# Two transformer blocks on one core: in block 1's attention the projections are dealt to the steps by a written plan, and the gating of an output moves ahead of them on VectorE

## The chip, the cores and the metric

One Trainium2 chip, one of its cores. The metric is the device time of one execution in microseconds. One execution was profiled; all rows come from it.

## What is computed

The reference runs two blocks on one sequence of 1024 tokens with 1024 features, each of two layers. The change touches the attention of block 1, which a layer has twice:

```python
def diff_attention(q, k, v, lam):            # branch "a": 4 heads of two halves of 64
    s = einsum(q, k) / sqrt(d); mask = kpos <= qpos
    p = softmax(s)
    pd = p[:, :, 0] - lam * p[:, :, 1]
    return einsum(pd, v)                     # then a norm, and the gate silu(z)
# branch "c": 8 heads of 64, partial_rope on q and k, three dilated windows
# whose outputs are mixed by their log-sums, then silu(z)
merged = einsum('bsnd,nbsd->bsd', sigmoid(gl), pb)
```

In both branches q and k are projections of the normed input, turned by `partial_rope`. gl are the merge gates, projections of the same input. The kernel folds branch c's three windows into one softmax with a mask that holds logarithms of multiplicities.

## The kernel before, in words

`Order` writes one list of units, and five programs, one for each engine (TensorE, ScalarE, VectorE, GpSimd, and SyncE for the DMAs), walk through the same list. Each program issues what a unit asks of its engine, in the order of the list, with waits on semaphores ahead. So the list sets the order on every engine, and on each the order is fixed.

**Projections.** A `proj` unit is 24 matmuls of 128x512 (8 tiles of K, three passes of split fp32r numbers, L1212) into one PSUM bank, for one half of the tokens. Two units share a chunk of weights. A chunk goes by DMA into one of 2 stages, and GpSimd splits it into a high and a low half (L2471, L2473) in one of 3 weight buffers. A unit that opens a chunk carries the load of the chunk two further on (`weight`, `upto`, `loads`).

**Attention.** A stage is one branch of one layer: 4 heads (pairs of heads in c) of 8 query blocks, 32 steps. Step s does, in this order:

- `scores(s + 1)`: TensorE, L1282 and L1283, into the four PSUM banks of pS. It waits for the rotated q and k.
- `turns(s)`: TensorE transposes the softmax's P (L1298), ScalarE copies it out (L1612). The first piece goes to the bank pt, the others to the two banks that rotate. In branch a only query blocks 4 to 7 have a second piece; in branch c every block has one or more.
- `soft(s + 1)`: VectorE adds the mask and takes the least (L2152), ScalarE takes the exponentials (L1603), and in branch a VectorE subtracts the second half (L2166).
- `fill`: projections from the list `fillers`, into the two rotating banks (`NARROW`). A unit takes the next bank and waits until what was in it has been read.
- `finish(s - 1)`: TensorE transposes the normed output into pt (L1319), VectorE multiplies it with the gate Z (L2183, the gating), which also frees pt for the next `turns`. For query blocks 3 and 7 ScalarE and VectorE then split Y into halves.
- `values(s)`: TensorE, L1311; ScalarE scales the output (in branch a after a mean on VectorE, L2173, and a power on GpSimd).

**The fillers of a head.** z0, z1 (the gate Z, a product on VectorE, L2012), v0, v1 with two transposes, some halves of merge gates (g; in branch a two for each head, in branch c four; ScalarE applies a tanh and the tile is stored to memory by SyncE), and the four of the next head's q0, q1, k0, k1. Those four are rotated by VectorE: a shuffle (L2023), the cosine product (L2027, which frees the bank), the sine product (L2030), a sum (L2033), then copies on ScalarE (L1557, L1560) and differences on VectorE (L2040, L2042). In heads 0 to 2, steps 0 to 5 hold one filler each, step 6 holds q0, q1, k0, k1 in a row (in branch c one gate tile behind them), and step 7 holds what is left: nothing in a, one gate tile in c. In the last head there are four fillers in a (steps 0, 4, 6, 7) and six in c (steps 0 and 3 to 7).

Of the kernel before, what the change touches and what calls it, by code (L numbers as in the profile page):

```python
# [24 lines left out]
P = 128  # L25
# [39 lines left out]
NR = 3  # L65
SHARE = {"a": (1, 1, 1, 1), "c": (2, 2, 2, 2)}
# [233 lines left out]
class Order:  # L300


    def __init__(self):
        self.units, self.weights, self.upto = [], [], []
# [18 lines left out]
    def add(self, u):  # L323
# [4 lines left out]
        if u.opens:  # L328
            u.box["c"] = self.weight(u, u.key, u.ahead)
        if u.box is not None:  # L330
            u["c"] = u.box["c"]
        if u.banked:
            u["bank"], u["free"] = self.take()
# [29 lines left out]
    def weight(self, u, key, ahead=None):  # L363
        self.weights.append(key)
        i = len(self.weights) - 1
        self.upto.append((u, i + (NR - 1 if ahead is None else ahead)))
        return i
# [64 lines left out]
    def first_block(self):  # L432
        self.put("start")
        self.put("load_x", i=0)
        self.upto.append((self.put("first_weights"), 1))
# [28 lines left out]
    def norm1(self, l, sums):  # L464
# [3 lines left out]
        self.upto.append((self.put("first_weights"), len(self.weights) + NR - 1))  # L468
# [34 lines left out]
    def mixing(self, l):  # L503
# [27 lines left out]
        def column(make, name, j, toks, emptied, ahead=None):  # L531
            box = {}
            sets = gate(j) if make == "gate_u" else gelu(toks, j)
            return self.in1(make, l, COL["b" + name] + j * P, j=j, box=box, sets=sets, emptied=emptied, ahead=ahead)

        v = [column("gelu_v", "v", j, vtok, "gelu", 2 - j if j < 3 else None) for j in range(4)]
# [80 lines left out]
    def attention(self, l, br):  # L617
# [9 lines left out]
        def qk_units(j, rel):  # L627
            def sets_of(name):
                def sets(u):
# [5 lines left out]
            return [u for name in "qk" for u in self.in1("qk", l, COL[br + name] + j * P, name=name, box={}, rel=rel,  # L635
                                                         scale=-SCALE1 if name == "q" else 1.0, sets=sets_of(name),
                                                         emptied="cosine")]
# [38 lines left out]
        self.run(qk_units(0, None))  # L676
# [4 lines left out]
        scored, softened, turned, valued = {}, {}, {}, {}  # L681
# [49 lines left out]
        def finish(s):  # L731
# [5 lines left out]
            self.pt_free = ("y_out", u.id)  # L737
            if g["qb"] % 4 == 3:
# [8 lines left out]
        share = SHARE[br]  # L747
        for s, (j, qb) in enumerate(steps):
# [24 lines left out]
        finish(s)  # L773
        self.fill(99)
# [63 lines left out]
    def norm2(self, l, rs):  # L838
# [3 lines left out]
        self.upto.append((self.put("first_weights"), len(self.weights) + NR - 1))  # L842
# [18 lines left out]
    def fourier_pool(self, l):  # L861
# [6 lines left out]
        f = [self.in2("f_copy", key("f", i), x=i, box={}, emptied="f_copy", ahead=NR - 1 - i) for i in range(2)]  # L868
# [2024 lines left out]
```

## Time and profile before

| | us |
|---|---|
| median of 3 runs | 4044.62 (4043.38 to 4048.3) |
| the profiled execution | 4042.67 |
| its span | 4040.9 |
| TensorE busy | 3743.9 |
| VectorE busy | 1718.9 |
| ScalarE busy | 1265.5 |
| GpSimd busy | 1091.6 |

The times of rows are microseconds from the start of the span unless they say ns. A branch a stage runs from about 372 to 691 in the first layer, a branch c stage from about 818 to 1208; the second layer's are alike. In a row `out<-in` names the tiles, x the count. What stands in square brackets is the idle time of the engine just ahead of the instruction, and what ended it. Ends of matmuls are modelled, and they overlap: a matmul of 128x512 is listed with 0.39 us where one starts every 0.23 us.

### The profile page before, as it was taken

To read this page: it belongs to the slowest core of one execution; us is meant where nothing else is said; L and a number is where in the kernel's file an instruction comes from. 1 tells how busy PE (TensorE), PEld (TensorE's weight loads), DVE (VectorE), ACT (ScalarE), POOL (GpSimd) and SP (SyncE) were. 2 spreads that over 40 slices of the span, in tenths; PEclk is the share of its full clock that TensorE was granted. 3 is DMA by queue.
4 is the path that set the end of the run, shared out by engine and by line. 5 is a ranking of instruction groups with operands and counts; after the bars stand their busy time and mean duration, and the time that the engine had idled before them with its cause. 6 is when DMAs were issued, how large, how long until landed. Compare 5 with 4: busy or idle time off the path is not lost.

```text
span 4040.9 us, 51127 instructions
## 1 busy us (share of the span) xinstructions
PE 3743.9 (93%) x20820; PEld 3311.2 (82%) x20820; DVE 1718.9 (43%) x3136; ACT 1265.5 (31%) x2868; POOL 1091.6 (27%) x806
## 2 busy tenths in 40 slices
PE   6999998999999899999899999968988998898898
PEld 5787777888887788777778888858988998898898
DVE  6624554433325552455443332554334334333333
ACT  3212443034331211244313333122245422134541
POOL 2533222321113362322231221326310023530002
PEclk9999999999999999999999999979989999998999
DMA  3111110401114212111130112322100031110012
GB/s 113 37 68 63 35 50 32 147 31 42 42 40 176 87 42 78 47 40 44 42 141 29 42 40 79 130 83 65 43 26 19 20 108 56 60 52 13 14 41 95
DMA packets 85195, 243.91 MB, mean 60 GB/s; under 512 B 10720, under 2 KB 25312, under 8 KB 84960
## 3 DMA queue, kind: packets, MB, share of 16 engines
q1 hardware_dynamic: 84960, 240.64, 17.4%
q8 instruction: 164, 2.69, 0.3%
q14 instruction: 71, 0.58, 0.0%
HBM read 190.07 MB, written 50.53 MB: 60 GB/s over the span
## 4 chain that ended last, share of the span: by engine, by line
PE 70%; DVE 14%; ACT 7%; issue 5%; DMA 2%; POOL 2%; SPq 1%; DVEq 0%; POOLq 0%; ACTq 0%
PE pj L1212 27%; PE pS L1212 21%; PE po L1420 4%; PE po L1311 4%; PE pS L1400 3%; PE pS L1402 2%; DVE tmp L2030 1%; PE pS L1282 1%; DVE KK L2042 1%; PE pS L1283 1%; PE pt L1298 1%; DVE tmp L2033 1%; ACT PT L1612 1%; PE pj L1386 1%; DVE tmp L2027 1%
## 5 line engine op out<-in xcount | busy, mean ns | idle before, releaser
L2471 POOL TENSOR_SCALAR Whi<-stage 128x1024 fp32r<-128x1024 f32 (+4 forms) x272 | 277.8, 1021 | 2138.9 <-DMA stage<-wstream 1328.4
L1212 PE MATMUL pj<-Hhi,Whi 128*128 128x512 f32 x1648 | 657.5, 399 | 8.3 <-DVE Hlo L1901 3.3
L1212 PE MATMUL pj<-Hhi,Wlo 128*128 128x512 f32 x1648 | 645.5, 392 | 0.0
L1212 PE MATMUL pj<-Hlo,Whi 128*128 128x512 f32 x1648 | 645.0, 391 | 0.0
L2473 POOL TENSOR_TENSOR Wlo<-stage,Whi 128x1024 fp32r<-128x1024 f32 (+4 forms) x272 | 621.9, 2287 | 22.7
L1212 PEld LDWEIGHTS pj<-Hhi,Whi 128*128 128x128 f32 x1648 | 311.6, 189 | 76.3 <-ACT PT L1612 6.6
L1212 PEld LDWEIGHTS pj<-Hhi,Wlo 128*128 128x128 f32 x1648 | 311.0, 189 | 66.8
L1212 PEld LDWEIGHTS pj<-Hlo,Whi 128*128 128x128 f32 x1648 | 311.6, 189 | 61.4
L1212 PE MATMUL pS<-Hhi,Whi 128*128 128x512 f32 x784 | 312.7, 399 | 12.2 <-DVE Hlo L1901 5.1
L1212 PE MATMUL pS<-Hlo,Whi 128*128 128x512 f32 x784 | 310.0, 395 | 0.0
L1212 PE MATMUL pS<-Hhi,Wlo 128*128 128x512 f32 x784 | 309.5, 395 | 0.0
L1311 PEld LDWEIGHTS po<-V,PT 128*128 128x128 f32 x1728 | 209.9, 197 | 7.8
L1311 PE MATMUL po<-V,PT 128*128 128x64 f32 (+1 forms) x1728 | 216.1, 278 | 0.0
L1212 PE MATMUL pS<-H2hi,Whi 128*128 128x348 f32 (+1 forms) x576 | 189.0, 328 | 19.2 <-POOL Wlo L2473 12.8
L1603 ACT ACTIVATE P<-P,st 128x128 f32<-128x128 f32 (+7 forms) x256 | 195.9, 772 | 4.2 <-DVE st L2152 4.1
L1212 PE MATMUL pS<-H2lo,Whi 128*128 128x348 f32 (+1 forms) x576 | 187.3, 325 | 0.0
L1212 PEld LDWEIGHTS pS<-Hhi,Whi 128*128 128x128 f32 x784 | 150.4, 192 | 44.8 <-DVE Hlo L1901 5.4
L1212 PE MATMUL pS<-H2hi,Wlo 128*128 128x348 f32 (+1 forms) x576 | 187.0, 325 | 0.0
L2405 DVE TENSOR_REDUCE st<-pS 116x1 f32<-116x1044 f32 (+1 forms) x72 | 89.7, 1246 | 216.5 <-PE pS L1402 216.5
L1212 PEld LDWEIGHTS pS<-Hhi,Wlo 128*128 128x128 f32 x784 | 150.1, 191 | 32.2
L1212 PEld LDWEIGHTS pS<-Hlo,Whi 128*128 128x128 f32 x784 | 150.4, 192 | 31.0
L1420 PE MATMUL po<-V,PT 116*116 116x128 f32 (+1 forms) x1296 | 166.0, 277 | 7.3 <-ACT PT L1816 5.2
(389 smaller groups left out, 7735.8 us busy)
## 6 DMA issues: line engine op xcount, KB each, us to landing
stage<-wstream SPq DMA_DIRECT2D x228, 512.0 KB, 4.3
merged<-Mb SPq DMA_DIRECT2D x32, 512.0 KB, 2.9
Mb<-merged SPq DMA_DIRECT2D x32, 512.0 KB, 5.1
gates<-tmp SPq DMA_DIRECT2D x48, 256.0 KB, 2.2
TH<-gates SPq DMA_DIRECT2D x24, 512.0 KB, 6.1
xres<-X SPq DMA_DIRECT2D x16, 520.0 KB, 5.7
xr<-xres SPq DMA_DIRECT2D x16, 520.0 KB, 4.6
X<-xT SPq DMA_DIRECT2D x16, 256.0 KB, 6.8
```

The source lines that it names most:

```text
L1212: x = pe.e.matmul(ps, w[a][:, v.koff + k * P:v.koff + k * P + P], moving(v.of, b, k, v.t0, v.n), start=k == 0 and i == 0, stop=k == v.K - ...
L1282: pe.e.matmul(out, m.QQ[h][:, qs], m.KK[h][:, c0:c0 + n], start=True, stop=False)
L1283: x = pe.e.matmul(out, m.QL[h][:, qs], m.KK[h][:, c0:c0 + n], start=False, stop=True)
L1298: x = pe.e.transpose(bank[:, i * P:i * P + P], p[:, (f + i) * P:(f + i) * P + P], ident[:, :])
L1311: x = pe.e.matmul(m.po[:, h * w:h * w + w], m.PT[buf][:, kb, :], v[:, kb, h * w:h * w + w], start=kb == 0, stop=kb == u.nb - 1)
L1400: pe.e.matmul(out, q[a][:, qs], m.kn[b][:, t], start=i == 0, stop=False)
L1402: x = pe.e.matmul(out, r[a][:, qs], m.KR[:, t], start=False, stop=a == 1)
L1420: x = pe.e.matmul(m.po[0:u.nq, 0:P], m.PT2[0:n, i, 0:u.nq], m.V2[u.h % 2][0:n, i, :], start=i == 0, stop=i == 8)
L1603: act.e.activation(p, p, ACT.Exp, bias=st[:, u.col + h:u.col + h + 1], scale=-1.0, accum_out=st[:, u.col + 2 + h:u.col + 3 + h]).then_inc( ...
L2405: dve.e.tensor_reduce(st[0:u.nq, u.col:u.col + 1], m.pS[0:u.nq, 0:1536].rearrange("p (c n) -> p c n", c=3)[:, :, 0:348], AX.XY, ALU.min).t ...
L2471: pool.e.tensor_scalar(upper, stage, 1.0, 0.0, ALU.mult, ALU.add).then_inc(*pool.tick("whi", c))
L2473: TT(lower, stage, upper.bitcast(F32), ALU.subtract).then_inc(*pool.tick("wlo", c))
```

## The change

The list of fillers gives way to a plan of eight slots for each head. Heads 0 to 2 of branch a: slot 0 k1 (of this head, held over) and z0; 1 z1; 2 v0; 3 v1; 4 a gate half; 5 q0 of the next head; 6 its k0 and a gate half; 7 its q1. (k1 is not there in head 0, whose q and k are done ahead of the steps.) Branch c is the same with two, four, four and six gate halves for the heads in place of four each: the middle heads have v0 and v1 in slot 2, gate halves in 3, 4 and 5 (ahead of q0) and 6. In the last head the gate halves are spread over slots 2 to 7: 2 and 5 in branch a, each of them in branch c.

`finish` keeps its place in the list, ahead of the slot's projections, but has only VectorE's and ScalarE's parts; TensorE's transpose is a unit of its own, `finish_turn`, behind them. q0 now waits for the scores of block 3, the others for those of block 7.

Loads of weights are placed anew all over the kernel: chunk c is loaded at the first projection behind the last use of chunk c - 3.

```diff
-SHARE = {"a": (1, 1, 1, 1), "c": (2, 2, 2, 2)}
+SHARE = {"a": (1, 1, 1, 1), "c": (1, 2, 2, 3)}
...
-        loaded = 0
-        for u, upto in self.upto:
-            last = min(upto, len(self.weights) - 1)
-            u["loads"] = range(loaded, last + 1)
-            loaded = max(loaded, last + 1)
+        at, behind = 0, [None] * len(self.units)
+        for u in reversed(self.units):
+            behind[u.id] = at
+            if u.kind in ("proj", "dft", "values_in", "first_weights"):
+                at = u.id
+        at = 0
+        for c in range(len(self.weights)):
+            at = max(at, self.first[c].id if c < NR else behind[self.used_at[c - NR]])
+            self.units[at].setdefault("loads", []).append(c)
...
-        self.run(qk_units(0, None))
+        (q0, q1), (k0, k1) = qk_units(0, {(x, i): None for x in "qk" for i in range(2)})
+        self.run([q0, q1, k0, k1])
...
+        held = []
+        def plan(j):
+            z = z_units(j)
+            g = gates[2 * sum(share[0:j]):2 * sum(share[0:j + 1])]
+            slots = [held + z[0:1], z[1:2], [], [], [], [], [], []]
+            held.clear()
+            if j == 3:
+                for i, u in enumerate(g):
+                    slots[2 + 6 * i // len(g)].append(u)
+                return slots
+            read = [[], []]
+            (q0, q1), (k0, k1) = qk_units(j + 1, {("q", 0): read[0], ("q", 1): read[1], ("k", 0): read[1], ("k", 1): read[1]})
+            held.append(k1)
+            reads.append(read)
+            v = v_units(j + 1)
+            v[1]["and_then"], g[0]["and_then"] = v[2], v[3]
+            others = v[0:2] + g[:-1]
+            for i, u in enumerate(others):
+                slots[2 + 4 * i // len(others)].append(u)
+            slots[5].append(q0)
+            slots[6] += [k0, g[-1]]
+            slots[7].append(q1)
+            return slots
...
             if qb == 0:
-                z, g = z_units(j), gates[2 * sum(share[0:j]):2 * sum(share[0:j + 1])]
-                v = v_units(j + 1) if j < 3 else []
-                if v:
-                    v[1]["and_then"], g[0]["and_then"] = v[2], v[3]
-                self.fillers += z + v[0:2] + g
+                amid = plan(j)
...
-            if qb == 6 and j < 3:
-                self.fill(len(self.fillers) % 2)
-                rel = [("scores", scored[s + 1].id, m) for m in range(2)]
-                self.fillers = qk_units(j + 1, rel) + self.fillers
-                self.fill(4)
-            if j < 3 or qb in (0, 4) or len(self.fillers) >= 8 - qb:
-                self.fill(1)
             if s:
                 finish(s - 1)
+            if j < 3 and qb in (3, 6):
+                reads[j][qb // 6] += [("scores", scored[s + qb // 6].id, h) for h in range(2)]
+            self.run(amid[qb])
+            if s:
+                self.put("finish_turn", of=finished[s - 1])
             values(s)
-            if qb == 7:
-                self.fill(99)
         finish(s)
-        self.fill(99)
+        self.put("finish_turn", of=finished[s])
...
-    def finish(u):
-        pe.wait_ge(u.normed)
-        pe.wait_ge(u.pt_free)
-        pe.e.transpose(m.pt[:, 0:P], m.ob[:, :], ident[:, :]).then_inc(*pe.tick("o_turned", u.id))
+    def finish_turn(u):
+        pe.wait_ge(u.of.normed)
+        pe.wait_ge(u.of.pt_free)
+        pe.e.transpose(m.pt[:, 0:P], m.ob[:, :], ident[:, :]).then_inc(*pe.tick("o_turned", u.of.id))
```

## Rows read from the trace of the kernel before

**Rows 1.** The page, part 1: engine, busy us, share of the span, instructions.
```profile
PE 3743.9 (93%) x20820; PEld 3311.2 (82%) x20820; DVE 1718.9 (43%) x3136; ACT 1265.5 (31%) x2868; POOL 1091.6 (27%) x806
```

**Rows 2.** Waits of TensorE, whole span: us in total, times, longest us.
```profile
PE pt L1298 <- DVE tmp L2183: 39.0, 26, 4.5
```

**Rows 3.** The same view for 800 to 1260, the first branch c stage.
```profile
PE pt L1298 <- DVE tmp L2183: 3.7, 7, 0.7
```

**Rows 4.** Timeline of TensorE, first change of head of branch a: start, us.
```profile
448.02 0.27 PE L1319 MATMUL pt<-ident,ob 128*128 128x128 f32 x1
...
450.49 0.30 PE L1282 MATMUL pS<-KK,QQ 128*128 128x128 f32 x1 [0.64 <-DVE KK L2042]
...
455.66 1.11 PE L1298 MATMUL pt<-ident,P 128*128 128x128 f32 x4 [4.53 <-DVE tmp L2183]
...
466.14 0.27 PE L1319 MATMUL pt<-ident,ob 128*128 128x128 f32 x1
...
468.06 0.41 PE L1298 MATMUL pt<-ident,P 128*128 128x128 f32 x2 [0.73 <-DVE tmp L2183]
468.23 0.48 PE L1212 MATMUL pj<-Hhi,Whi 128*128 128x512 f32 x1
```

**Rows 5.** Windows: stretch, length, busy by engine, granted clock, DMA share, GB/s.
```profile
448.00:460.60 12.60, 7.43 (x51) 6.76 (x49) 7.60 (x20) 5.49 (x15) 0.74 (x2) 0.86 0.01 2
640.00:657.00 17.00, 10.95 (x52) 9.12 (x53) 10.34 (x33) 8.69 (x27) 2.95 (x8) 0.80 0.00 1
1142.00:1152.00 10.00, 8.27 (x58) 6.89 (x58) 5.43 (x18) 6.65 (x21) 0.00 (x0) 1.00 0.01 2
```

**Rows 6.** The chain that ended last, in order of time: start, us, what.
```profile
820.85 7.03 PE pj L1212 x24
829.46 5.58 PE pj L1212 x24
```

**Rows 7.** Timeline of TensorE, first change of head of branch c.
```profile
909.63 0.27 PE L1319 MATMUL pt<-ident,ob 128*128 128x128 f32 x1
...
912.79 0.31 PE L1282 MATMUL pS<-KK,QQ 128*128 128x128 f32 x1
...
922.06 0.27 PE L1319 MATMUL pt<-ident,ob 128*128 128x128 f32 x1
...
931.92 0.27 PE L1319 MATMUL pt<-ident,ob 128*128 128x128 f32 x1
...
933.78 0.41 PE L1298 MATMUL pt<-ident,P 128*128 128x128 f32 x2 [0.44 <-DVE tmp L2183]
...
934.16 0.48 PE L1212 MATMUL pj<-Hhi,Whi 128*128 128x512 f32 x1
```

**Rows 8.** Timeline of VectorE, the same change of head.
```profile
922.37 0.29 DVE L2183 SCALAR_TENSOR_TENSOR tmp<-pt,Z 128x128 f32<-128x128 f32 x1 [4.07 <-PE pt L1319]
...
933.35 0.28 DVE L2183 SCALAR_TENSOR_TENSOR tmp<-pt,Z 128x128 f32<-128x128 f32 x1
...
934.94 0.55 DVE L2152 CUSTOM_DVE_ANT_0 P<-pS,mC 128x384 f32<-128x384 f32 x1
```

**Rows 9.** Timeline of VectorE, rotation of k0, first change of head of branch a.
```profile
445.39 0.74 DVE L2023 STREAM_SHUFFLE tmp<-pj 128x512 f32<-128x512 f32 x1
446.16 0.69 DVE L2027 SCALAR_TENSOR_TENSOR tmp<-pj,cos 128x512 f32<-128x512 f32 x1
```

**Rows 10.** Timeline of VectorE, a softmax of 384 keys in branch a.
```profile
641.72 0.55 DVE L2152 CUSTOM_DVE_ANT_0 P<-pS,mA 128x384 f32<-128x384 f32 x1
...
645.70 0.34 DVE L2183 SCALAR_TENSOR_TENSOR tmp<-pt,vec,Z 128x128 f32<-128x128 f32 x1
```

**Rows 11.** Timeline of TensorE, end of the first branch a stage.
```profile
690.76 0.36 PE L1319 MATMUL pt<-ident,ob 128*128 128x128 f32 x1 [2.04 <-ACT ob L1623]
690.84 0.71 PE L1212 MATMUL pS<-Hhi,Whi 128*128 128x512 f32 x1
```

**Rows 12.** Instructions on the tile KK: count, ns least/median/most, first and last start.
```profile
L2042 DVE TENSOR_TENSOR KK<-tmp,KK x64: 684/687/2774, 365.0 to 2425.9; 64x512 fp32r<-64x512 f32 x64
```

More of the change, by code:

```diff
@@ L303, in __init__ @@
     def __init__(self):
-        self.units, self.weights, self.upto = [], [], []
+        self.units, self.weights, self.first, self.used_at = [], [], [], {}
         self.bank, self.banks, self.bank_free = 0, WIDE, [None] * 6
@@ L328, in add @@
         if u.opens:
-            u.box["c"] = self.weight(u, u.key, u.ahead)
+            u.box["c"] = self.weight(u.key)
         if u.box is not None:
             u["c"] = u.box["c"]
+            if u.ends:
+                self.used_at[u.c] = u.id
         if u.banked:
@@ L361, in take, with weight @@
         return b, self.bank_free[b]
-    def weight(self, u, key, ahead=None):
+    def weight(self, key):
         self.weights.append(key)
-        i = len(self.weights) - 1
-        self.upto.append((u, i + (NR - 1 if ahead is None else ahead)))
-        return i
+        return len(self.weights) - 1
     def phase(self):
@@ L434, in first_block @@
         self.put("load_x", i=0)
-        self.upto.append((self.put("first_weights"), 1))
+        self.first += [self.put("first_weights")] * 2
         self.put("load_x", i=1)
@@ L467, in norm1 @@
         rs, = self.spread(sums)
-        self.upto.append((self.put("first_weights"), len(self.weights) + NR - 1))
+        u = self.put("first_weights")
+        if l == 0:
+            self.first.append(u)
         self.norm(of, 0, range(2), rs, self.x_ready[0], self.h_free[0])
@@ L529, in gate, with column @@
             return sets
-        def column(make, name, j, toks, emptied, ahead=None):
+        def column(make, name, j, toks, emptied):
             box = {}
             sets = gate(j) if make == "gate_u" else gelu(toks, j)
-            return self.in1(make, l, COL["b" + name] + j * P, j=j, box=box, sets=sets, emptied=emptied, ahead=ahead)
-        v = [column("gelu_v", "v", j, vtok, "gelu", 2 - j if j < 3 else None) for j in range(4)]
+            return self.in1(make, l, COL["b" + name] + j * P, j=j, box=box, sets=sets, emptied=emptied)
+        v = [column("gelu_v", "v", j, vtok, "gelu") for j in range(4)]
         self.together([v[0][0], v[1][0], v[2][0]], self.inside)
@@ L634, in sets_of @@
                 return sets
-            return [u for name in "qk" for u in self.in1("qk", l, COL[br + name] + j * P, name=name, box={}, rel=rel,
-                                                         scale=-SCALE1 if name == "q" else 1.0, sets=sets_of(name),
-                                                         emptied="cosine")]
+            units = [self.in1("qk", l, COL[br + name] + j * P, name=name, box={}, scale=-SCALE1 if name == "q" else 1.0,
+                              sets=sets_of(name), emptied="cosine") for name in "qk"]
+            for pair in units:
+                for u in pair:
+                    u["rel"] = rels[u.name, u.i]
+            return units
         def v_units(j):
@@ L737, in finish @@
             self.pt_free = ("y_out", u.id)
+            finished[s] = u
             if g["qb"] % 4 == 3:
@@ L867, in fourier_pool @@
         self.put("small_in", l=l)
-        f = [self.in2("f_copy", key("f", i), x=i, box={}, emptied="f_copy", ahead=NR - 1 - i) for i in range(2)]
-        p = [self.in2("p_copy", key("p", i), x=i, box={}, emptied="p_copy", ahead=i * (NR - 1)) for i in range(2)]
+        f = [self.in2("f_copy", key("f", i), x=i, box={}, emptied="f_copy") for i in range(2)]
+        p = [self.in2("p_copy", key("p", i), x=i, box={}, emptied="p_copy") for i in range(2)]
         self.together([f[0][0], f[1][0], p[0][0]], self.inside)
@@ L1439, in tensor_program @@
     parts = {"phase": phase, "proj": proj, "sums": sums, "spread": spread, "ln": ln, "lnmix": lnmix, "v_turn": v_turn,
-             "scores": scores, "turns": turns, "values": values, "finish": finish, "gmix": gmix, "amix": amix, "dft": dft,
+             "scores": scores, "turns": turns, "values": values, "finish_turn": finish_turn, "gmix": gmix, "amix": amix, "dft": dft,
              "mark3": mark3, "pool_out": pool_out, "values_in": values_in, "scores2": scores2, "turns2": turns2,
```

10 lines of the change are left out of this document (6 added, 4 removed).

## The prediction

> **What bounds the kernel now.** I read the page first: TensorE is busy for 3743.9 of 4040.9 us, 93% [rows 1]. Nothing takes its place unless it becomes late by much, so what the change is worth is what it removes from, or adds to, TensorE's idle time in the four attention stages (A and C, in two layers; the change gives no engine more or less work). The waits view names the one idle time that the change aims at: the transposes of P wait 39.0 us in 26 places for VectorE's gating (L2183), up to 4.5 us each [rows 2]; one C stage has 3.7 us of it [rows 3], so one A stage has 39.0 / 2 - 3.7 = 15.8.
>
> The timeline of TensorE at a change of head in A shows where. Step 6 issues q0, q1, k0, k1 in a row; VectorE needs some 5 to 6 us for each, as long as TensorE, and the gating of the last output stands behind all four. TensorE does values(6), waits 0.64 us for KK, does the scores, then waits 4.53 us for the gating; a step later it waits 0.73 us again [rows 4]. The windows view adds the clock: 0.86 granted over those 12.6 us [rows 5], so 3.5 us at 1.2 instead of 2.4 GHz, a loss of some 1.5 us. **Removable in A: 0.64 + 4.53 + 0.73 + 1.5 = 7.4 us per change of head**, three per stage. In C a gate tile stood as a fifth behind the four, and one change of head costs only 3.7 / 3 = 1.2 us.
>
> **What the change does to the order.** VectorE's part of finish(s-1) now stands ahead of the step's projections, but TensorE's transpose of the same output (finish_turn) stays behind them. VectorE takes its instructions in the order written, so it waits at the gating until TensorE has run the whole step's projections, and the rotation of a key waits with it. With one projection in a step this costs nothing: VectorE would have waited for that projection anyway. In two slots there are two: slot 6 (k0, then a gate tile) and slot 0 of the next head (k1, then z0). There the rotation of k0 or k1 starts one projection (5.58 us, [rows 6]) later than it could.
>
> **New wait 1, scores of the next head on k0.** Count from the start of the transpose L1319. Gating starts 0.31 us later (922.37 against 922.06, where VectorE had waited 4.07 us for just this) [rows 7, 8] and its slot on VectorE is 0.27. From the shuffle of k0 to the first score matmul that needs it: 450.49 - 445.39 = 5.10 us [rows 4, 9]. Ready at 0.31 + 0.27 + 5.10 = 5.7. TensorE would be there, values(6) in between, at 450.49 - 448.02 - 0.64 = 1.8 in A [rows 4] and at 912.79 - 909.63 = 3.2 in C [rows 7]. **Stall 3.9 us in A, 2.5 in C.**
>
> **New wait 2, z1 on the bank.** Two PSUM banks rotate. Slot 0 comes with finish(7), whose gating is followed by the split of Y: from the gating to VectorE's next instruction 934.94 - 933.35 = 1.59 us [rows 8]. So k1's shuffle starts at 0.31 + 1.59 = 1.9, and its cosine product, which frees k1's bank, ends 446.16 + 0.69 - 445.39 = 1.46 later [rows 9], at 3.4. In A the transposes of steps 0 to 3 use no bank of the two, z1 takes k1's: it starts at 3.5 instead of 468.23 - 466.14 - 0.73 = 1.4 [rows 4]. **Stall 2.1 us in A.** In C every step's transposes take a bank: turns(1) gets k1's and z1 gets that of z0, whose product on VectorE (0.69 us, taken as for the cosine product of the same shape [rows 9]) stands behind all of k1's rotation, the 5.10 us: 1.9 + 5.10 + 0.69 = 7.7, or 7.65 without the rounding up. Undisturbed, z1 starts at 934.16 - 931.92 - 0.44 = 1.8 (0.44 was the wait for the gating) [rows 7]. **Stall 5.85 us in C**, some 1.9 of it before the second half of turns(1), the rest before z1.
>
> **New wait 3, A only.** The maxima of scores(2) stand behind z0's product, at 7.6; from the first mask to the end of the gating behind the softmax it takes 645.70 + 0.34 - 641.72 = 4.3 us [rows 10], so turns(2) can go at 11.9. TensorE, z1 done at 9.1, is there at about 10.6. **1.3 us.** In C there are no such 4.3 us (no subtraction) and a late z1: nothing.
>
> **Clock.** After a gap of 2.04 us the first matmul of the next stage took 0.71 us against 0.48 for the same shape [rows 11, 4], and 24 matmuls behind a broken stretch took 7.03 us against 5.58 [rows 6]: 1.5 us. I charge 1.5 us to each new gap of 2 us or more: two per change of head in A (3.9, 2.1) and two in C (2.5, 5.85). The bound below is nothing for all four. The Trainium skill ("TensorE: Matmul & The Clock Gate", What's actually happening) says the opposite: the ramp penalty is under 1% of a typical span and is not to be fitted. By that rule the clock is left out on both sides and the sum below would be +47 instead of +74. Here the rows are against it, since these gaps recur at every head.
>
> **Shares and bare steps.** A step without a projection shows the softmax's latency. In A there are four of them in the last head before (steps 1, 2, 3, 5) and four after (3, 4, 6, 7); 17 us with three of them hold 6.05 us of idle at clock 0.80 [rows 5], so about 3 us each, in either place: nothing. In C the share 1, 2, 2, 3 fills the last head's two bare steps; 10 us with both hold 1.7 us of idle [rows 5]: -2 us a stage, -4 in all. Projections, DMAs and splits are the same in number. Weight loads are now issued at the first unit behind the last use of their buffer; one chunk was loaded at each opening before, right behind that same use, so I cost this at nothing: it is hidden as long as a chunk is there one projection (5.58 us) before its use, and each keeps a step or more. Bounds -3 and +3 us. The one queue that it moves past is the store of the gate tile of slot 6 on SP: the next z's load waits there until ScalarE has done that tile, behind k0's copies, and z0 comes only after q1 and k1, over 15 us later.
>
> **Sum.** A: 3.9 + 2.1 + 1.3 + 3.0 = 10.3 against 7.4 removed, +2.9, six changes of head: +17. C: 2.5 + 5.85 + 3.1 = 11.4 against 1.2, +10.2, six times: +61. Bare steps -4. **+74 us** on the profiled execution's own 4042.67, 4116.7; the median of the runs, 4044.62, lies 2 us above it: **4118.6**.
>
> **Rivals.**
> (a) *Faster: VectorE rotates k0 and k1 while the tile behind them runs.* For it: 4.53 us of the wait sits exactly where the title of the change points, and q1 now fills step 7, which had nothing. It decides if the transpose is on TensorE ahead of the second projection, or if its output is ready so early that the order on VectorE does not bind. Then waits 1 to 3 vanish, A gains 6 x 7.4 = 44, C up to 6 and bare steps 4: 3991. Against it: the diff puts finish_turn behind run(amid[qb]). 10%.
> (b) *Only wait 1 (and 3) comes true*, the bank rotation leaving z1 free, or the two-in-a-slot steps being fewer than I read ("one per step" taken at its word). A: 3.9 + 1.5 + 1.3 - 7.4 = -0.7; C: 2.5 + 1.5 - 1.2 = +2.8; six each, less 4: +9, 4053. 10%.
> (c) *Worse: GpSimd's weight splits fall into the k rotations.* One low half of KK took 2.77 us where the median is 0.69 [rows 12]. If that hits each of the twelve first waits, +2.1 x 12 = +25: 4144. Against it: the next load is held behind the gate tile's store, so its split runs beside q1. The Trainium skill ("SBUF — State Buffer", SBUF: two separate sides) has the rule: VectorE with two SBUF inputs and GpSimd lock each other out for a whole instruction. By it this rival would be worth about one split each time; the maximum in the row agrees, how often it happens here is open. 6%.
> The forecast has 74%.
>
> **How the numbers follow.** About 0.2%, 8 us, is what a measurement can tell from no change. The forecast's own range: without any of the new clock losses 4118.6 - 6 x 6 = 4082, and a few us of loads below and above. Taking in (c) the range reaches 4148; below I go to 4070, which leaves (a), (b) and nothing else outside. Faster 0.10 from (a); (b) at 4053 lies on the edge of no change: same 0.04; slower 0.86.
>
> **What would show it.** In the profile after: the 39.0 us of waits on L2183 nearly gone; new waits of L1282 on KK, six of nearly 4 us and six of 2.5; waits of L1212 on VectorE's Z or cosine product, and of turns on the cosine product in C; the clock under 1 there; VectorE idle ahead of L2183 for two projections in slots 6 and 0. A C stage longer by some 30 us, an A stage by 8. No wait on KK above 1 us would make the whole prediction wrong; KK waits without waits of z1 would be (b).

## The result, and the profile after

The changed kernel takes 4112.65 us (median of 4 runs, 4105.64 to 4116.72); the kernel before, run beside it, 4045.98 (4 runs). The ratio is **1.0164** with a 95% interval of 1.0148 to 1.018, so the change costs about 66.7 us, where 74 were forecast. Run again beside the experiments it took 4111.83 against 4036.21 us, 1.0191 (1.0178 to 1.0204). The profiled execution took 4111.37 us.

The page of the kernel after: its span, and the busy time of each engine, to be read against [rows 1].

```profile
span 4109.6 us, 51077 instructions
...
PE 3774.0 (92%) x20820; PEld 3337.7 (81%) x20820; DVE 1681.5 (41%) x3136; ACT 1265.2 (31%) x2868; POOL 1089.4 (27%) x806
```

The number of instructions on each engine is the same. The span grew from 4040.9 to 4109.6, by 68.7 us. TensorE's busy time grew by 30.1 of these with not one matmul more, and its idle time by the other 38.6. So a good 40% of the loss is the same work done at a lower clock: the granted clock fell from 0.964 to 0.955 as a mean over the span.

Where it went is read by stage. A stage is measured from its first score matmul to its last output transpose (L1319 before, L1354 after):

| us | A, layer 1 | C, layer 1 | A, layer 2 | C, layer 2 |
|---|---|---|---|---|
| before | 318.34 | 390.09 | 318.07 | 390.45 |
| after | 321.10 | 422.94 | 319.80 | 422.62 |
| difference | +2.8 | +32.9 | +1.7 | +32.2 |
| of it TensorE busy | +3.8 | +12.9 | +1.7 | +11.9 |
| of it TensorE idle | -1.0 | +20.0 | +0.1 | +20.2 |

The four differences make 69.5 us, all of the 68.7; outside the stages the two kernels differ by under 1 us in sum. Nearly all of the loss lies in branch C.

The waits of TensorE over the whole span, those that the change makes or takes away (us in total, times, longest):

```profile
PE pS L1317 <- DVE KK L2077: 34.9, 12, 3.7
PE pj L1247 <- DVE Z L2047: 22.3, 6, 3.7
...
PE pj L1333 <- ACT PT L1647: 14.0, 26, 1.3
PE pj L1247 <- DVE tmp L2062: 11.5, 6, 1.9
PE pj L1333 <- DVE tmp L2062: 10.3, 6, 1.7
...
PE pt L1333 <- DVE tmp L2218: 3.9, 4, 1.0
```

The last line is what became of the 39.0 us in 26 places [rows 2]: the wait that the change aims at is all but gone, 3.9 us. In its place stand the scores of the next head on KK (12 times: twelve changes of head), z1 on VectorE's product Z (6 times), z1 on the cosine product (6) and the second half of turns(1) on the cosine product (6). These four make 79.0 us.

The timeline of TensorE at the first change of head of branch a (start, us, what, and in brackets the wait before it), for [rows 4]:

```profile
434.00 0.27 PE L1354 MATMUL pt<-ident,ob 128*128 128x128 f32 x1
...
439.53 0.45 PE L1317 MATMUL pS<-KK,QQ 128*128 128x128 f32 x1 [3.70 <-DVE KK L2077]
440.41 1.07 PE L1333 MATMUL pt<-ident,P 128*128 128x128 f32 x4
...
466.08 0.58 PE L1247 MATMUL pj<-Hhi,Whi 128*128 128x512 f32 x1 [1.91 <-DVE tmp L2062]
...
474.74 0.49 PE L1333 MATMUL pt<-ident,P 128*128 128x128 f32 x3
```

The transposes of P at 440.41 follow the scores at once, where they waited 4.53 us before; but the scores themselves came 3.70 us late, and z1 1.91. The transposes at 474.74 do not wait at all.

VectorE at the same place:

```profile
434.31 0.35 DVE L2218 SCALAR_TENSOR_TENSOR tmp<-pt,vec,Z 128x128 f32<-128x128 f32 x1 [2.37 <-PE pt L1354]
434.58 0.73 DVE L2058 STREAM_SHUFFLE tmp<-pj 128x512 f32<-128x512 f32 x1
...
437.98 1.40 DVE L2077 TENSOR_TENSOR KK<-tmp,KK 64x512 fp32r<-64x512 f32 x2 [0.70 <-ACT KK L1592]
```

This is the whole of the mechanism in three lines. VectorE stood idle for 2.37 us at the gating until the transpose of 434.00, although k0 had been in its bank for a whole projection; the shuffle that begins k0's rotation came right behind; KK was ready 5.4 us after the start of the transpose, and TensorE, with only values(6) to do, waited for it.

TensorE at a change of head of branch c, for [rows 7]:

```profile
900.16 0.44 PE L1317 MATMUL pS<-KK,QQ 128*128 128x128 f32 x1 [2.12 <-DVE KK L2077]
...
926.37 0.28 PE L1354 MATMUL pt<-ident,ob 128*128 128x128 f32 x1
...
929.72 0.41 PE L1333 MATMUL pj<-ident,P 128*128 128x128 f32 x2 [1.72 <-DVE tmp L2062]
...
933.84 0.80 PE L1247 MATMUL pj<-Hhi,Whi 128*128 128x512 f32 x1 [3.71 <-DVE Z L2047]
```

and VectorE beside it, for [rows 8]:

```profile
926.68 0.29 DVE L2218 SCALAR_TENSOR_TENSOR tmp<-pt,Z 128x128 f32<-128x128 f32 x1 [5.70 <-PE pt L1354]
...
928.29 0.72 DVE L2058 STREAM_SHUFFLE tmp<-pj 128x512 f32<-128x512 f32 x1
...
933.10 0.69 DVE L2047 SCALAR_TENSOR_TENSOR Z<-tmp,pj 128x512 f32<-128x512 f32 x1
```

VectorE is idle for 5.70 us, one whole projection, ahead of the gating. Then k1's rotation begins, its cosine product frees k1's bank for turns(1) at 929.72, and z0's product, last in the queue, frees z0's bank for z1 at 933.84.

The clock, by the windows view (stretch, length, busy by engine, granted clock, DMA share, GB/s), over the first change of head in A and the slot 0 to 1 stretch in C, and two lines of the chain that ended last (start, us, what):

```profile
434.00:450.00 16.00, 12.30 (x58) 10.67 (x57) 6.96 (x19) 4.64 (x12) 4.17 (x4) 0.79 0.33 101
926.00:941.00 15.00, 9.57 (x40) 7.57 (x39) 6.67 (x15) 4.86 (x12) 0.00 (x0) 0.77 0.09 32
```

```profile
829.88 5.59 PE pj L1247 x24
...
933.84 7.43 PE pj L1247 x24
```

The same 24 matmuls take 5.59 us where TensorE had been kept busy and 7.43 behind the gaps of slots 0 and 1.

### The profile page after: what moved, and what is told of

The parts are those of the page before. It is cut to its first block, busy times and chain, and to the rows that moved or that the text cites. A ratio compares the mean times of both kernels' runs of the same rounds, so it can differ in the third digit from the quotient of the medians.

```text
span 4109.6 us, 51077 instructions
## 1 busy us (share of the span) xinstructions
PE 3774.0 (92%) x20820; PEld 3337.7 (81%) x20820; DVE 1681.5 (41%) x3136; ACT 1265.2 (31%) x2868; POOL 1089.4 (27%) x806
## 4 chain that ended last, share of the span: by engine, by line
PE 76%; DVE 11%; ACT 6%; issue 3%; DMA 2%; POOL 2%; SPq 0%; DVEq 0%; POOLq 0%; ACTq 0%
PE pj L1247 33%; PE pS L1247 21%; PE po L1455 4%; PE po L1346 3%; PE pS L1435 3%; PE pS L1437 2%; PE pS L1317 2%; PE pS L1318 1%; PE pt L1333 1%; DVE tmp L2068 1%; DVE KK L2077 1%; PE pj L1421 1%; ACT PT L1647 1%; PE pj L1333 1%; DMA stage<-wstream 1%
## 5 line engine op out<-in xcount | busy, mean ns | idle before, releaser
L1247 PE MATMUL pj<-Hhi,Whi 128*128 128x512 f32 x1648 | 671.6, 408 | 42.6 <-DVE Z L2047 22.3
L1247 PE MATMUL pj<-Hlo,Whi 128*128 128x512 f32 x1648 | 656.2, 398 | 0.0
L1247 PE MATMUL pj<-Hhi,Wlo 128*128 128x512 f32 x1648 | 654.8, 397 | 0.0
L1317 PE MATMUL pS<-KK,QQ 128*128 128x512 f32 (+3 forms) x384 | 143.9, 381 | 37.4 <-DVE KK L2077 34.9
```

The source lines that it names most:

```text
L1247: x = pe.e.matmul(ps, w[a][:, v.koff + k * P:v.koff + k * P + P], moving(v.of, b, k, v.t0, v.n), start=k == 0 and i == 0, stop=k == v.K - ...
L1317: pe.e.matmul(out, m.QQ[h][:, qs], m.KK[h][:, c0:c0 + n], start=True, stop=False)
```

## The experiments

Twelve kernels were run. Unless said otherwise each is the kernel after with one edit. The theory: VectorE, held at the gating until the slot's second projection is done, makes k0 and k1 late (waits 1 and 2), and TensorE's clock falls behind the new gaps. The rivals: the loads' new places or the new shares cost the time; the order within a slot is to blame and not the gating; the new plan of slots is bad wherever the gating stands. Here are their stages, in the order A, C, A, C:

| us | A1 | C1 | A2 | C2 |
|---|---|---|---|---|
| 1 gating behind both | 328.76 | 411.26 | 326.56 | 409.63 |
| 2 gating between | 316.96 | 394.87 | 315.09 | 395.43 |
| 3 slot 6 turned round | 326.67 | 427.94 | 329.35 | 424.51 |
| 4 slot 0 turned round | 324.77 | 412.42 | 323.85 | 409.57 |
| 5 old shares | 321.55 | 421.30 | 319.70 | 419.22 |
| 6 before, loads only | 319.18 | 390.12 | 318.13 | 388.93 |
| 7 another plan | 336.70 | 405.01 | 338.03 | 403.67 |
| 8 after, again | 321.62 | 422.28 | 319.87 | 419.56 |
| 9 second plan | 310.92 | 405.03 | 311.22 | 404.06 |
| 10 its gating ahead | 333.06 | 415.71 | 331.72 | 414.56 |
| 11 second plan in A only | 313.66 | 388.54 | 313.46 | 389.54 |
| 12 its gating behind | 342.83 | 388.53 | 341.04 | 389.47 |

### 1. The gating behind the slot's projections, as it stood before

```diff
-            if s:
-                finish(s - 1)
             if j < 3 and qb in (3, 6):
...
             self.run(amid[qb])
+            if s:
+                finish(s - 1)
             if s:
                 self.put("finish_turn", of=finished[s - 1])
```

> The kernel after, with VectorE's gating put back behind all projections of a step. Theory (VectorE stands at the gating until TensorE has run the step's projections, and the rotation of k0 and k1 waits with it): the waits of L1317 on KK go from 34.9 us to under 4, those of z1 on Z from 22.3 to under 4. In their place the gating is late again behind q0 and q1, one in a step: about 3 us in A and 2 in C at turns(6), about 4 and 2 at turns of the next head. A as long as now, C some 6 us shorter for each change of head: about 4075 us. Rival (the new waits come from the plan itself, one projection of cover being too little for a rotation of 5.1 us, wherever the gating stands): KK waits stay at 3.7 and 2.1 us each, the gating's waits come on top, slower than 4112.

Measured: 4099.2 us (4096.96 to 4104.87), 1.0155 (1.014 to 1.017) of the kernel before. TensorE's waits, first line:

```profile
PE pt L1333 <- DVE tmp L2218: 85.6, 38, 3.7
```

The waits on KK and of z1 on Z are gone altogether, and the gating's wait is back and more than twice the 39.0 of before. By stage: C is shorter by 11.7 and 13.0 us, A longer by 7.7 and 6.8. So the mechanism of waits 1 and 2 stands, but this edit is no clean removal of it: the gating behind a rotation costs nearly as much elsewhere. The expected 4075 us was missed by 24, and A was to stay as long as it was.

### 2. The gating between the two projections of a slot

```diff
-            if s:
-                finish(s - 1)
...
-            self.run(amid[qb])
+            now = amid[qb]
+            first = 1 if len(now) > 1 and now[0].make == "qk" else 0
+            self.run(now[:first])
+            if s:
+                finish(s - 1)
+            self.run(now[first:])
```

Only slots 6 and 0 are touched: there k0 or k1 is rotated ahead of the gating, and the other projection's work stays behind it.

> The kernel after, with VectorE's gating behind the first and ahead of the second projection where a slot holds a key's projection and another (slot 6: k0, gating, gate tile; slot 0: k1, gating, z0), ahead of the projections elsewhere, as now. Theory: the rotation of 5.1 us runs while the second projection's 5.6 us do; KK waits under 2 us in all, z1 waits under 1 us each in C, no clock falls at changes of head, and the gating is early behind q0 and q1. A stages some 29 us shorter (about 292), C stages some 29 shorter (about 393): about 3995 us, faster than both kernels. Rival (plan itself): KK waits stay, about 4112.

Measured: 4043.09 us (10 runs), 1.0014 (1.0005 to 1.0024). **Between 61 and 71 us come back** (1.0164 or 1.0191 less 1.0014, by 4037.11) with the gating's place in two slots, which no rival about loads, shares or the plan allows for. It is not the 3995 that was expected, a miss by 48 us: the kernel is as fast as the one before, not faster. Two timelines of this kernel say why. TensorE:

```profile
439.71 0.30 PE L1320 MATMUL pS<-KK,QQ 128*128 128x128 f32 x1 [0.97 <-DVE KK L2080]
...
465.18 0.66 PE L1336 MATMUL pt<-ident,P 128*128 128x128 f32 x2 [4.00 <-DVE tmp L2221]
```

VectorE and GpSimd:

```profile
457.76 0.74 DVE L2061 STREAM_SHUFFLE tmp<-pj 128x512 f32<-128x512 f32 x1
...
458.99 2.77 DVE L2068 TENSOR_TENSOR tmp<-tmp,sin 128x512 f32<-128x512 f32 x1
...
464.68 0.35 DVE L2221 SCALAR_TENSOR_TENSOR tmp<-pt,vec,Z 128x128 f32<-128x128 f32 x1
```

```profile
458.82 2.38 POOL L2511 TENSOR_TENSOR Wlo<-stage,Whi 128x1024 fp32r<-128x1024 f32 x1
```

The wait on KK fell from 3.70 to 0.97. But q1's rotation in slot 7, a softmax and k1's rotation stand one behind the other on VectorE, so k1 begins only at 457.76, meets a weight split of GpSimd (2.77 us for a product that takes 0.69 undisturbed), and the gating behind it is 4.00 us late. Of the old wait of 39.0 us in 26 places three quarters are left, 29.4 us in 14 places.

### 3. and 4. The order within a slot

```diff
-            slots[6] += [k0, g[-1]]
+            slots[6] += [g[-1], k0]
```

> The kernel after, with slot 6 holding the gate tile first and k0 last. Theory: VectorE begins k0's rotation behind finish_turn in either order, so having k0 first buys nothing: KK waits stay 34.9 us within 3, time 4112 within 8. Rival (k0's rotation is at least partly hidden by the tile behind it, and the wait is what is left): the waits grow by up to the 5.6 us of a projection each, twelve times, up to 4180.

Measured: 4135.98 us (4131.67 to 4141.07), 1.0245 (1.0229 to 1.026): 23 us more than the kernel after (22 by the ratio of experiment 8), where none was expected. The waits on KK:

```profile
PE pS L1317 <- DVE KK L2077: 57.5, 12, 6.5
```

and the place itself, VectorE, GpSimd and TensorE:

```profile
441.16 2.63 DVE L2068 SCALAR_TENSOR_TENSOR tmp<-tmp,tmp 128x512 f32<-128x512 f32 x1
...
446.04 0.45 PE L1317 MATMUL pS<-KK,QQ 128*128 128x128 f32 x1 [5.71 <-DVE KK L2077]
```

```profile
440.60 2.65 POOL L2508 TENSOR_TENSOR Wlo<-stage,Whi 128x1024 fp32r<-128x1024 f32 x1
```

This is rival (c) of the prediction, brought about by the edit. With the gate tile first, its store on SP comes earlier, and the next load, issued 0.4 us behind the store in both kernels, with it: at 435.43, 3.1 us ahead of the transpose, in place of 439.61, 5.6 us behind it. So the split falls into k0's rotation; in the kernel after it runs at 444.36, beside q1. The sum of the rotation took 2.63 us in place of 0.69, and the wait grew from 3.70 to 5.71. At each of the twelve changes of head some operation of k0's rotation is stretched to 1.9 us or more; the waits on KK are 5.7 to 6.5 us in A and 3.3 to 3.8 in C.

```diff
-            slots = [held + z[0:1], z[1:2], [], [], [], [], [], []]
+            slots = [z[0:1] + held, z[1:2], [], [], [], [], [], []]
```

> The kernel after, with slot 0 holding z0 first and k1 last. Theory (in C z1 takes the bank of the slot's second projection and turns(1) that of the first; in A z1 takes the first): in C turns(1) waits for z0's product only, z1 for k1's cosine product, at 4.1 us behind L1354 in place of 7.5; in A z1 waits for z0's product, 2.7 in place of 3.3. Six times -3.4 in C and -0.6 in A, and some of the clock falls there go: 4085 us, between 4075 and 4090. KK waits unchanged. Rival (z1 is late for another cause, its weights or the split of Y): no change, 4112.

Measured: 4098.34 us (4094.1 to 4101.2), 1.015 (1.0133 to 1.0167) of the kernel before. The expected 4085 us (at most 4090) was missed. Each C stage is 10 us shorter than in experiment 8, the kernel after once more, and that was expected: z0's product now stands ahead of k1's rotation, so z1's bank is free early, and the wait on Z falls from 22.3 to 7.7 us. That is **wait 2 in C shown by one pair turned round**, with the waits on KK unchanged at 34.9 us. In A a small gain was expected and 3 to 4 us were lost per stage. The timeline of TensorE in A:

```profile
466.37 0.50 PE L1247 MATMUL pj<-Hhi,Whi 128*128 128x512 f32 x1 [1.29 <-DVE Z L2047]
...
476.42 0.52 PE L1333 MATMUL pt<-ident,P 128*128 128x128 f32 x3 [1.79 <-DVE tmp L2218]
```

z1 still waits 1.29 us, now for z0's product, and wait 3, absent in the kernel after, appears with 1.79.

### 5., 6. and 8. Shares, loads, and the kernel after once more

```diff
-SHARE = {"a": (1, 1, 1, 1), "c": (1, 2, 2, 3)}
+SHARE = {"a": (1, 1, 1, 1), "c": (2, 2, 2, 2)}
```

> The kernel after, with branch C's gate halves dealt 4, 4, 4, 4 again instead of 2, 4, 4, 6. Theory (the shares only fill two bare steps of the last head, about 2 us a stage): some 4 us slower than the kernel after, all in the C stages. Rival (the heavier last head or the lighter first one costs time in C): the C stages get shorter, up to 30 us each.

Measured: 4105.72 us, 1.0176 (1.0162 to 1.0189). The kernel after itself had 4111.83 beside it (experiment 8). The C stages differ by 1.0 and 0.3 us, in favour of the old shares. Some 4 us more than the kernel after were expected, and 6 us less were measured, with intervals that overlap: the new shares bring nothing that can be told.

Experiment 6 is the kernel before with only the new places of the loads:

```diff
-        loaded = 0
-        for u, upto in self.upto:
...
+        for c in range(len(self.weights)):
+            at = max(at, self.first[c].id if c < NR else behind[self.used_at[c - NR]])
+            self.units[at].setdefault("loads", []).append(c)
```

> The kernel before, with only the new placement of the weight loads (chunk c behind the last use of chunk c - 3), attention as before. Theory: no effect, within 3 us of before. Rival (splits at new places collide with VectorE or come late): up to the whole difference of 67 us.

Measured: 4037.64 us (12 runs), 1.0002 (0.9993 to 1.001). With the attention as before, the loads' new places are worth nothing, and the rival is out in that form. What they do together with a new order of the slots is seen in experiments 3 and 7.

> The kernel after, unchanged, beside the other runs on this chip and with its trace: ratio to before 1.0164 within 0.002. It is the reference for the three others.

Measured: 4111.83 us (4109.75 to 4117.21), 1.0191 (1.0178 to 1.0204). That is 0.0027 above the first session's ratio, more than the 0.002 allowed for, and the two intervals for the same pair of kernels barely overlap (the upper end of the first is 1.018); here the kernel before had 4036.21, 10 us below the first session. Differences of under 0.3% between sessions are therefore not read.

### 7. A plan with one projection between a rotation and the next

```diff
-            slots = [held + z[0:1], z[1:2], [], [], [], [], [], []]
+            slots = [z[0:1], held[:], [], [], [], [], [], []]
...
+            slots[3] += v[0:2]
+            slots[4].append(q0)
+            slots[5] += g[0:1]
+            slots[6] += [k0, g[1]]
```

The gating goes between, as in 2. This kernel changes one part of the computation: q0's rotation in slot 4 overwrites the tile that holds v1 before it is transposed, so V is another one; the number and shape of the instructions are the same.

> A plan made from what the first four showed: gating ahead of the projections, but between the two where a slot starts with a key's; never two rotations in neighbouring steps where it can be helped: z0 | k1 | z1 | v0, v1 | q0 of the next head | gate half | k0, gate half | q1; in C the second gate chunk in slots 1 and 2; in A's last head z0, k1, nothing, z1, nothing, gate, nothing, gate. Theory (in e2 the waits moved to turns(1) because VectorE had q1's rotation, a softmax and k1's rotation in a row): that wait of 4.0 us goes, A stages 300 to 308 us where before has 318, C stages about 391: 10 to 30 us under before, about 4015. Rival (VectorE's work around the change of head is too long for any order): A stays at 317 and the time at before's, within 8 us.

Measured: 4107.02 us (4104.57 to 4114.88), 1.0181 (1.0167 to 1.0194): a miss by 90 us. TensorE in A, and GpSimd beside it:

```profile
458.51 0.80 PE L1257 MATMUL pj<-Hhi,Whi 128*128 128x512 f32 x1 [8.32 <-POOL Wlo L2518]
```

```profile
454.21 0.55 POOL L2559 TENSOR_TENSOR st<-st,vec 128x1 f32<-128x1 f32 x1 [11.71 <-DVE st L2218]
...
454.99 1.04 POOL L2516 TENSOR_SCALAR Whi<-stage 128x1024 fp32r<-128x1024 f32 x1
456.12 2.34 POOL L2518 TENSOR_TENSOR Wlo<-stage,Whi 128x1024 fp32r<-128x1024 f32 x1
```

z0 waits 8.32 us for its own weights, and it is not the DMA that is late: the load was issued at 440.28, 0.4 us behind the gate tile's store, and had landed at 444.73. The split of these weights stands on GpSimd behind the power of values(7) (L2559), which waited 11.71 us for VectorE's mean; the mean came late, behind q1's rotation. The split came there by the new rule for the loads. Chunk c is loaded and split at the first projection behind the last use of chunk c - 3, and with q0 taken ahead of the gate half, chunk c - 3 of z0's is the q chunk, last used by q1 in slot 7: so z0's chunk is split at z0 itself. In the kernel after it is split at q1 (444.36), ahead of values(7), and z0 stands one projection further back. All six such waits in the A stages look the same, 8.3 us each, 49.9 in all; the other two of the eight in TensorE's waits (55.2 us) are not of this plan: the kernel before has two as well, 5.6 us.

### 9. and 10. A second plan, and the position of the gating in it

The plan spreads the rotations and takes the first z of the next head into slot 6, with its weights asked for early:

```diff
-            slots = [held + z[0:1], z[1:2], [], [], [], [], [], []]
+            slots = [z[1:2], held[:], [], [], [], [], [], []]
...
+            slots[2] += v[0:2]
+            slots[3] += g[0:-2] or g[0:1]
+            slots[4] += g[-2:-1] if len(g) > 2 else []
+            slots[4].append(q0)
+            slots[5] += g[-1:]
+            slots[6] += [k0, z[0]]
...
+            now = amid[qb]
+            first = 1 if len(now) > 1 and now[0].make == "qk" else 0
```

Experiment 10 differs from it in one line:

```diff
-            first = 1 if len(now) > 1 and now[0].make == "qk" else 0
+            first = 0
```

> A second plan, with no z tile waiting for fresh weights at the change of head and no tile's rotation overrun by VectorE's backlog: for each head z1 | k1 | v0, v1 | gate half | q0 of the next head | gate half | k0, its z0 | q1, with the gating between the two of slot 6 and ahead of all elsewhere; in A's last head z1, k1, gate halves in 4 and 6. Theory (a rotation needs a step or a tile behind it before TensorE asks for it, a wait of z0 on GpSimd's split as in e7 is gone since its chunk is loaded behind a gate half two steps earlier): A stages 298 to 306 us (before 318), C stages 388 to 393 (before 390): 20 to 40 us under before. Rival (whatever the order, VectorE's softmax and rotations make some 7 us of waits at each change of head, as in before, after and e2): within 8 us of before.

> The same plan with the gating ahead of both projections of slot 6 too, as the change has it. Theory: k0's rotation waits for finish_turn again; KK waits of some 3.9 us in A and 2.1 to 2.5 in C and a slower clock behind them come back at each of twelve changes of head, and nothing else: 35 to 60 us over e9. Rival (the gating order doesn't matter, only what stands where): the time of e9 within 8 us.

Measured: 4059.4 us (1.0056, 1.0042 to 1.007) with the gating between, **4119.69** (1.0202, 1.0189 to 1.0216) with it ahead. The first was expected 20 to 40 us under the kernel before and came out 21 over it; the second lies 60 over the first, at the end of what was expected. In TensorE's waits of the second:

```profile
PE pS L1327 <- DVE KK L2087: 34.9, 12, 3.7
```

This line, to the tenth of a microsecond the one of the kernel after, does not exist in the kernel with the gating between. One line of order costs 60 us: 22.1 and 20.5 in the A stages, 10.7 and 10.5 in the C stages. So the cost of wait 1 holds under another plan; in A it is much larger here than in the kernel after, and the clock is why: of the 22.1 us in the first A stage 12.5 are the same matmuls taking longer (TensorE busy 296.63 for 284.14 us), with a granted clock of 0.94 for 0.98. Experiment 2 had 0.95 in its A stages already, and so had less to lose.

The plan by itself gives A stages 7 us under those before, but C stages 14 to 15 us over, where none was expected. In C, TensorE:

```profile
870.27 0.44 PE L1343 MATMUL pj<-ident,P 128*128 128x128 f32 x2 [3.36 <-ACT PT L1657]
```

The transposes wait for ScalarE to copy P out of the bank, and ScalarE has q0's copies ahead of that.

### 11. and 12. The second plan in A alone

In C projections and gating stand as in the kernel before, with the shares 2, 2, 2, 2; in A the second plan, its last head's gate tiles in slots 2 and 6. Experiment 12 puts the gating of every step of A behind all projections:

```diff
-                first = 1 if len(now) > 1 and now[0].make == "qk" else 0
+                first = len(now)
```

> The second plan in branch A only (its last head's gate halves in slots 2 and 6 instead of 4 and 6), with C's projections and gating exactly as before the change. Theory (the second plan took 7 us off each A stage and put 15 on each C stage, where the four rotations in a row with a gate tile behind them cost next to nothing, and q0 in an earlier slot held ScalarE's copies of P up): A stages 306 to 311 us, C stages 390: 15 to 25 us under before, faster than both kernels. Rival (A's gain was borrowed from the C stage behind it): within 8 us of before.

> The same, with VectorE's gating in A behind all projections of a step, as before the change. It prices what the change wanted from moving the gating. Theory: behind q0, q1 and k1 (a rotation of 5 to 6 us each) the gating is late and turns waits 2 to 4 us for it, nine times a stage, some with a slower clock: A stages 10 to 25 us longer than in e11, C the same. Rival (the place of the gating is worth nothing once rotations stand alone): the time of e11 within 8 us.

Measured: 4031.36 us (12 runs, 4029.59 to 4039.05), **0.9979** (0.997 to 0.9987) of the kernel before; and 4082.78 (4078.4 to 4085.22), 1.01 (1.0086 to 1.0115). The first beats both kernels, by 9 us over the one before, which is just at what can be told from no change. It is not the gain of 15 to 25 us that was expected: its A stages are 4.6 us shorter than those of before, where 7 to 12 were reckoned, its C stages 1 to 1.5. The waits of TensorE in the first A stage, of 11 and then of 12:

```profile
PE pt L1382 <- ACT PT L1675: 11.3, 7, 4.1
PE pt L1361 <- DVE tmp L2246: 7.4, 4, 2.2
PE pt L1361 <- DVE st L2236: 4.7, 5, 1.2
```

```profile
PE pt L1361 <- DVE tmp L2246: 23.7, 10, 3.6
PE pt L1361 <- DVE st L2236: 13.6, 6, 3.9
PE pt L1382 <- ACT PT L1675: 6.1, 4, 2.4
```

With the gating behind, an A stage is 28 to 29 us longer, where 10 to 25 were expected. The edit moves the gating in every step of A, but the new waits stand where the forecast of the experiment put them: nine in the stage, 3.1 us at the transposes behind slot 4 (q0), 3.6 behind slot 7 (q1) and 3.9 behind slot 1 (k1), 32 us in all, and none behind slots 2 and 6, which hold two. In this plan the idea of the change is therefore a good one where a step has a single projection that is rotated; what it loses in the kernel after, it loses in the two slots that have two.

## Why the prediction was right

The forecast named the direction, the mechanism and nearly the size (+74, measured +66.7). That the size came so near is in part luck: A was forecast too high and the clock in C too low, and the two take from each other. By its own steps:

**What is removed.** The 39.0 us of waits on the gating fell to 3.9, as expected; the first KK wait of 0.64 us turned into 3.70.

**New wait 1** was right in both branches: 3.70 us in A for 3.9, 2.12 in C for 2.5. From the transpose to the scores it took 439.53 - 434.00 = 5.53 us for the 5.7 reckoned. Experiment 2 takes it away (0.97 left), and experiment 10 brings it back, 34.9 us in 12 places.

**New wait 2** was right in both: 1.91 for 2.1 in A; in C 1.72 + 3.71 = 5.43 for 5.85, and z1 starts 933.84 - 926.37 = 7.47 us after the transpose for the 7.65 reckoned (its own terms make 7.69). Experiment 4 shows the bank's part in C by turning one pair round. It is the largest single piece of the loss.

**New wait 3** (1.3 us) did not come. The chain on VectorE was reckoned well: the gating ended 474.22 + 0.35 - 462.76 = 11.8 us after the transpose, for 11.9. But TensorE came to turns(2) only at 12.0 instead of 10.6, since z1, at the lower clock, took over 7 us instead of 5.58. The step had summed a stall and a clock loss that lie side by side, where the longer of the two counts. In experiment 4 the clock was 1.00 at this place, TensorE came at 11.0, and the wait was there, with 1.79 us (0.8 of it from a subtraction that met a split on GpSimd and took 1.40 us in place of 0.62).

**Clock.** By idle and busy time the forecast divides like this. Its waits and bare steps: in A 3.9 + 2.1 + 1.3 against 5.9 removed, in C 8.35 against 1.2, six each, less 4, make +47 us; its clock terms, 1.5 more per head in A and 3.1 in C (two gaps at 1.5 would be 3.0), +28. Measured were 38.6 us more idle and 30.1 us more busy with the same matmuls. The clock term is thus right in sum, but not by branch: per stage 4.5 us were forecast in A, where 3.8 and 1.7 came, and 9.3 in C, where 12.9 and 11.9 did. A matmul's end in the trace is modelled; their starts are not, and they say the same. One projection matmul starts 0.23 us behind the other at 2.4 GHz and 0.43 at 1.2; 86 were of the second kind before and 186 are after, all of the difference in the four stages, at 0.2 us each 20 of the 30 us. The Trainium skill ("TensorE: Matmul & The Clock Gate", What's actually happening) puts the ramp penalty at under 1% of a typical kernel span and advises not to fit a specific count of cold matmuls. The forecast read from it that the clock would be left out, which is more than the page says. The 30 us added here are 0.7% of the span, so the figure itself is not contradicted; but they are over 40% of the change, and without them the forecast would have read +47.

**Bare steps and shares** (-4 us) were wrong in a small way: experiment 5 gives nothing for them, even a little the other way. The idle time in the bare steps' rows was read as time that a projection would fill. Filling them takes gate tiles from the slots of other heads, and those may have become bare in turn; that is a guess that was not tried.

**Loads** at nothing: right, 1.0002 in experiment 6. But the forecast looked at SP's queue alone, and two other things hang on where a load stands: what the split meets on VectorE (experiment 3, 23 us) and what stands ahead of the split on GpSimd (experiment 7, 49.9 us of waits).

**A sum** of +2.9 per change of head came out as 0.6 to 0.9 (2.8 and 1.7 us over three), **C** of +10.2 as 10.7 to 11.0. Per A stage that is 6 to 7 us too much. The missing wait 3 makes 3.9 of them, waits 1 and 2 with 3.70 and 1.91 for 3.9 and 2.1 another 1.2, and the rest is mostly the clock. In C the idle time came out at +20 us a stage for the 19.5 reckoned, waits that were a little smaller against the bare steps' gain that was missing, and the clock term is what was too small. The wait of one slot's transposes on ScalarE's copies (1.31 us at 883.19, behind q0's) was not seen ahead; waits of this kind were 9.8 us over the whole span before and are 14.0 after.

**The rivals.** (a) would have needed the gating's order not to bind; experiments 2 and 10 show that it binds. (b) falls with the waits of z1. (c) did not happen in the kernel after, for the reason given (the split runs beside q1), and did in experiment 3, with +1.9 us per wait on average (57.5 less 34.9 over twelve) where 2.1 was its price.

What stays open: why experiment 1, with the gating where it stood before, is still 62 us slower than the kernel before. Its waits on the gating sum to 85.6 us; which part is the plan of slots and which the separate transpose was not tried. Also whether a C plan exists that gains: experiment 9's C stages lose 14 us, and C then stayed as before.

## What to carry to other kernels

On an engine that takes its instructions in order, an operation moved ahead moves its wait ahead too: ask what the operation waits for, and count everything that stands behind it from that moment on. Price a slot by its fullest case: the gating ahead of the steps with a single rotated projection gained 28 us an A stage here, ahead of two in two slots it cost 60 us over the kernel. Putting it between the two won that back, but by itself no more: with it the changed plan was as fast as the kernel before. Where two buffers rotate, follow which operation frees the one that the next projection takes; turning one pair round in that slot was worth 10 us a stage in C, and cost 3 to 4 in A, where the banks fall otherwise. And when work is dealt anew, look at each queue that the weights pass through: in experiment 7 they lay in the stage for 10 us, because their split stood behind an operation that waited for VectorE.

## What was not expected of the hardware

A VectorE operation that reads two tiles of SBUF and meets a split on GpSimd ends only when the split is over: a tensor_tensor of 128x512 took 2.77 us beside a split of 2.38 (experiment 2), a scalar_tensor_tensor 2.63 beside one of 2.65 (experiment 3), each ending some 0.55 us behind the split's end, where such an operation takes 0.69 otherwise. The Trainium skill ("SBUF — State Buffer", SBUF: two separate sides) states the lock; the trace agrees. What surprised was how little moves it: turning round two projections of one slot brought it onto the critical rotation and cost 23 us.

In C a gap costs more by the clock than was reckoned: over the 16 and 15 us that begin with the transpose and hold gaps of 3.7 (A) and of 1.7 and 3.7 us (C) the granted clock was 0.79 and 0.77, a mean over time at 2.4 and at 1.2 GHz, and 24 matmuls took 7.4 us instead of 5.6, while the waits before them were themselves right to half a microsecond.
